# Sums of squares in the mixer: one float32 product, or two rounded ones

## The reference

```python
def l2_normalize(t):
    tf = t.astype(jnp.float32)
    return tf * lax.rsqrt(jnp.sum(tf * tf, axis=-1, keepdims=True) + NORM_EPS)

gdn_qkv = jax.nn.silu(causal_dwconv(gdn_qkv, gdn_conv_w))
g_q, g_k, g_v = [t.reshape(Bsz, S, GDN_HEADS, GDN_HEAD_DIM) for t in jnp.split(gdn_qkv, 3, axis=-1)]
g_q = l2_normalize(g_q) * (GDN_HEAD_DIM ** -0.5)
g_k = l2_normalize(g_k)
# then k k^T and q k^T by chunks of 64 tokens, a triangular inverse of 64x64 blocks, and a scan over 4 chunks
```

## Time and profile before

| | |
|---|---|
| median of 3 runs | 1473.48 us (1473.37 to 1474.0) |
| the profiled execution's own time | 1473.31 us |
| its span | 1471.5 us |
| TensorE busy | 1462.2 us (99%) |
| VectorE, ScalarE, GpSimd busy | 956.8 (65%), 822.2 (56%), 216.1 (15%) |
| granted TensorE clock, mean | 0.998 |
| the four old products of a layer start at | 219.07, 221.34, 231.75, 234.02 (layer 0), 755.41 for the first of layer 1 |
| gram products start at | 241.80 and 778.14 |

### The profile page before, as it was taken

One profiled execution on the slowest core, in us unless ns is written; L12 is line 12 of the kernel. 1 busy time (PEld: TensorE's weight loads), 2 busy tenths in 40 slices (PEclk: granted clock), 3 DMA queues, 4 the chain that ended last, 5 costly groups with the idle time before them and its releaser, 6 DMA issues.

```text
span 1471.5 us, 29397 instructions
## 1 busy us (share of the span) xinstructions
PE 1462.2 (99%) x12785; PEld 1414.7 (96%) x12785; DVE 956.8 (65%) x1394; ACT 822.2 (56%) x1268; POOL 216.1 (15%) x126
## 2 busy tenths in 40 slices
PE   9999999999999999999999999999999999999998
PEld 9999999999999989999999999999989999999997
DVE  6655377786655475655558685655478767677766
ACT  6554377655544365544476655554476675565762
POOL 1000143113000261000332040000430001400001
PEclk9999999999999999999999999999999999999999
DMA  9655464237555456555553256555555344653341
GB/s 384 243 196 184 166 229 144 99 107 263 183 197 201 164 216 229 200 186 190 199 177 140 69 200 218 189 201 196 176 215 201 115 144 166 209 189 139 132 156 58
DMA packets 40239, 267.43 MB, mean 182 GB/s; under 512 B 4464, under 2 KB 4976, under 8 KB 10032
## 3 DMA queue, kind: packets, MB, share of 16 engines
q1 hardware_dynamic: 38592, 260.39, 49.9%
q0 software_dynamic: 944, 4.38, 0.8%
q10 hardware_dynamic: 576, 0.79, 0.2%
HBM read 264.49 MB, written 1.05 MB: 180 GB/s over the span
## 4 chain that ended last, share of the span: by engine, by line
PE 98%; DVE 1%; DMA 0%; ACT 0%; POOL 0%; issue 0%; SPq 0%
PE PS L602 19%; PE PS L604 19%; PE PS L603 19%; PE PS L596 6%; PE PS L598 6%; PE PS L597 6%; PE PS L636 4%; PE PS L635 4%; PE PS L638 4%; PE PS L676 1%; PE PS L1321 1%; PE PS L1044 1%; PE PS L1339 1%; PE PS L1331 1%; PE PS L1352 1%; PE PS L1361 0%
## 5 line engine op out<-in xcount | busy, mean ns | idle before, releaser
L602 PE MATMUL PS<-xTH,WH 128*128 128x256 f32 x2256 | 637.8, 283 | 0.0
L604 PE MATMUL PS<-xTH,rawL 128*128 128x256 f32 x2256 | 624.9, 277 | 0.0
L603 PE MATMUL PS<-xTL,WH 128*128 128x256 f32 x2256 | 624.9, 277 | 0.0
L2065 DVE TENSOR_TENSOR rawL<-raw,WH 128x1024 fp32r<-128x1024 f32 (+1 forms) x407 | 495.0, 1243 | 104.7 <-ACT WH L1488 103.8
L1488 ACT ACTIVATE WH<-raw 128x1024 fp32r<-128x1024 f32 (+2 forms) x477 | 484.5, 1046 | 133.5 <-PE PS L638 98.1
L602 PEld LDWEIGHTS PS<-xTH,WH 128*128 128x128 f32 x2256 | 423.9, 188 | 7.8 <-issue 5.3
L603 PEld LDWEIGHTS PS<-xTL,WH 128*128 128x128 f32 x2256 | 423.8, 188 | 2.6 <-issue 1.9
L604 PEld LDWEIGHTS PS<-xTH,rawL 128*128 128x128 f32 x2256 | 424.5, 188 | 0.0
L2767 POOL TENSOR_TENSOR rawL<-raw,WH 128x1024 fp32r<-128x1024 f32 (+3 forms) x71 | 166.7, 2375 | 767.7 <-ACT WH L1488 767.7
L1568 ACT ACTIVATE sg<-PS 128x256 f32<-128x256 f32 x79 | 30.3, 383 | 168.2 <-PE PS L604 168.2
L635 PE MATMUL PS<-WH,hTH 128*128 128x256 f32 x512 | 122.4, 276 | 0.0
(11 more groups left out here) (424 smaller groups left out, 2183.5 us busy)
## 6 DMA issues: line engine op xcount, KB each, us to landing
raw<-in_weights SPq DMA_DIRECT2D x232, 1024.0 KB, 4.8
gb<-in_lngb SPq DMA_DIRECT2D x16, 512.0 KB, 5.3
raw<-in_weights SPq DMA_DIRECT2D x2, 1056.0 KB, 4.9
raw<-in_weights SPq DMA_DIRECT2D x4, 512.0 KB, 5.4
gb<-in_ln SPq DMA_DIRECT2D x4, 512.0 KB, 4.9
cst<-in_consts POOLq DMA_DIRECT2D x1, 1378.5 KB, 10.0
raw<-in_weights SPq DMA_DIRECT2D x4, 256.0 KB, 5.0
xt<-in_x POOLq DMA_DIRECT2D x1, 1024.0 KB, 17.5
```

The lines of the kernel that those rows point to most:

```text
L602: e.matmul(out, u.H(i, c0, 128), xH, start=first, stop=False)
L603: e.matmul(out, u.H(i, c0, 128), xL, start=False, stop=False)
L604: return e.matmul(out, u.L(i, c0, 128), xH, start=False, stop=end)
L2065: e.tensor_tensor(u.L(i, 0, w), u.R(i, w), u.H(i, 0, w).bitcast(F32), ALU.subtract).then_inc(*low_dve.up(k))
```

## The change

The squares are split like the weights. ScalarE copies `sq` rounded to `sqH` (`square_high`), VectorE subtracts `sq - sqH` into `sqL` (`square_low`), and TensorE multiplies ones (rounded, `onesF`, cast once per layer by VectorE) by sqH and then by sqL into the same bank. The order moves too: on TensorE the four `squares` stand two, three, one and two quarters later; on ScalarE `norm("q", 1)` stands ahead of `rounds("v", 0, 2)` instead of behind it.

```diff
@@ -363,7 +363,8 @@
     decay_act, decay_vec, decays_summed = [signal(n) for n in ("decay_act", "decay_vec", "decays_summed")]
     conv_begun, conv_done, conv_act = [signal(n) for n in ("conv_begun", "conv_done", "conv_act")]
     masks, level_masked = signal("masks"), signal("level_masked")
-    squares_summed, norm_scale, unit_length = [signal(n) for n in ("squares_summed", "norm_scale", "unit_length")]
+    squares_high, squares_low, squares_summed, norm_scale, unit_length = [
+        signal(n) for n in ("squares_high", "squares_low", "squares_summed", "norm_scale", "unit_length")]
     gram_product, gram_masked, tokens_turned, tokens_scaled = [
         signal(n) for n in ("gram_product", "gram_masked", "tokens_turned", "tokens_scaled")]
     inverse_product, inverse_copied, inverse_updated = [signal(n) for n in ("inverse_product", "inverse_copied", "inverse_updated")]
@@ -458,6 +459,9 @@
         m.kq = put("kq", [128, 4, 2, S], 0)
         m.cv = [put("cva", [128, 2, S], 8), put("cvb", [128, 2, S], 10)]
         m.sq = [put("sqa", [128, 512], 12), put("sqb", [128, 512], 14)]
+        m.sqH = [put("sqHa", [128, 512], 44, F32R), put("sqHb", [128, 512], 46, F32R)]
+        m.sqL = [put("sqLa", [128, 512], 48, F32R), put("sqLb", [128, 512], 50, F32R)]
+        m.onesF = put("onesG", [128, 128], 52, F32R)
         m.rs = [put("rsa", [128, 512], 16), put("rsb", [128, 512], 61)]
         m.eb = put("eb", [128, 2, 4, 128], 18)
         m.Es, m.Eu, m.df = [put(n, [128, 8, 64], k) for n, k in (("Es", 22), ("Eu", 24), ("df", 26))]
@@ -898,7 +902,7 @@
         def mix(p, nxt, l):
             m = mix_buffers(l)
             s = ring[0]
-            kq, cv, sq, U, T, Z, Bs, Eu, wq, ez, zb = m.kq, m.cv, m.sq, m.U, m.T, m.Z, m.Bs, m.Eu, m.wq, m.ez, m.zb
+            kq, cv, U, T, Z, Bs, Eu, wq, ez, zb = m.kq, m.cv, m.U, m.T, m.Z, m.Bs, m.Eu, m.wq, m.ez, m.zb
 
             def A(key, off, *freed_by):
                 bank[key] = order[(s + off) % 4]
@@ -983,8 +987,9 @@
 
             def squares(nm, i, b):
                 B(("squares", l, nm, i), b, (norm_scale, (l, nm, i, "ln")))
-                e.wait_ge(*conv_act.at((l, nm, i, "sq")))
-                e.matmul(PS[:, b, :], ones, sq[i][:, :], start=True, stop=True).then_inc(*squares_summed.up((l, nm, i)))
+                e.wait_ge(*squares_low.at((l, nm, i)))
+                e.matmul(PS[:, b, :], m.onesF[:, :], m.sqH[i][:, :], start=True, stop=False)
+                e.matmul(PS[:, b, :], m.onesF[:, :], m.sqL[i][:, :], start=False, stop=True).then_inc(*squares_summed.up((l, nm, i)))
 
             for q in range(3):
                 quarter("k", 1, q)
@@ -992,20 +997,22 @@
             quarter("q", 0, 0)
             quarter("q", 0, 1)
             quarter("q", 0, 2)
+            quarter("q", 0, 3)
+            quarter("q", 1, 0)
             squares("k", 0, 7)
-            quarter("q", 0, 3)
-            squares("k", 1, 4)
-            quarter("q", 1, 0)
             quarter("q", 1, 1)
             quarter("q", 1, 2)
+            squares("k", 1, 4)
             quarter("q", 1, 3)
             quarter("v", 0, 0)
             quarter("v", 0, 1)
             quarter("v", 0, 2)
+            quarter("v", 0, 3)
             squares("q", 0, 5)
-            quarter("v", 0, 3)
+            quarter("v", 1, 0)
+            quarter("v", 1, 1)
             squares("q", 1, 6)
-            for q in range(4):
+            for q in range(2, 4):
                 quarter("v", 1, q)
             quarter("z", 0, 0)
 
@@ -1692,6 +1699,10 @@
                     e.wait_ge(*squares_summed.at((l, "k", i)))
                 e.activation(m.sq[i][:, :].rearrange("p (j s) -> p j s", j=2), dst, ACT.Square).then_inc(*conv_act.up((l, nm, i, "sq")))
 
+            def square_high(nm, i):
+                e.wait_ge(*conv_act.at((l, nm, i, "sq")))
+                e.activation(m.sqH[i][:, :], m.sq[i][:, :], ACT.Copy).then_inc(*squares_high.up((l, nm, i)))
+
             def norm(nm, i):
                 r = m.rs[i]
                 e.wait_ge(*squares_summed.at((l, nm, i)))
@@ -1722,22 +1733,26 @@
             rounds("k", 1, 2)
             conv_end("k", 0)
             conv_first("k", 1)
+            square_high("k", 0)
             rounds("q", 0, 0)
             conv_end("k", 1)
             rounds("q", 0, 2)
             conv_first("q", 0)
+            square_high("k", 1)
             rounds("q", 1, 0)
             conv_end("q", 0)
             rounds("q", 1, 2)
             conv_first("q", 1)
+            square_high("q", 0)
             rounds("v", 0, 0)
             conv_end("q", 1)
+            square_high("q", 1)
             table(TBL_LN_EXP)
             norm("k", 0)
             norm("k", 1)
             norm("q", 0)
+            norm("q", 1)
             rounds("v", 0, 2)
-            norm("q", 1)
             rounds("v", 1, 0)
             rounds("v", 1, 2)
             rounds("z", 0, 0)
@@ -2293,6 +2308,10 @@
                     ins = e.scalar_tensor_tensor(v, v, 128 ** -0.5, r3, op0=ALU.mult, op1=ALU.mult)
                 ins.then_inc(*unit_length.up((l, nm, i)))
 
+            def square_low(nm, i):
+                e.wait_ge(*squares_high.at((l, nm, i)))
+                e.tensor_tensor(m.sqL[i][:, :], m.sq[i][:, :], m.sqH[i][:, :].bitcast(F32), ALU.subtract).then_inc(*squares_low.up((l, nm, i)))
+
             def decayed_q(t):
                 e.wait_ge(*unit_length.at((l, "q", 1)))
                 e.tensor_tensor(m.eb[:, t, :, :], m.eb[:, t, :, :], kq[:, :, 1, 128 * t:128 * t + 128], ALU.mult)
@@ -2312,6 +2331,7 @@
                     *tokens_scaled.up((l, "k", t)))
 
 
+            e.tensor_copy(m.onesF[:, :], ones)
             lows("k", 0, 0)
             lows("k", 0, 2)
             e.wait_ge(*decays_summed.at(l))
@@ -2333,13 +2353,17 @@
             lows("k", 1, 0)
             lows("k", 1, 2)
             conv("k", 1)
+            square_low("k", 0)
             lows("q", 0, 0)
             lows("q", 0, 2)
+            square_low("k", 1)
             conv("q", 0)
             lows("q", 1, 0)
             lows("q", 1, 2)
             conv("q", 1)
+            square_low("q", 0)
             lows("v", 0, 0)
+            square_low("q", 1)
             unit_norm("k", 0)
             unit_norm("k", 1)
             unit_norm("q", 0)
```

## The result

The changed kernel takes 1475.88 us (median of 22 runs, 1475.22 to 1476.66) against 1473.32 for the kernel before on the same chip (22 runs, one of which took 4173.26 us and doesn't move the median): ratio 1.0018, 95% interval 1.0012 to 1.0024. The forecast was 1475.8. So the change costs some 2.6 us (0.18%), though by the forecast's price it takes 3.2 us of work off TensorE. The profiled execution takes 1476.25, its span 1474.1 (before: 1473.31 and 1471.5).

The account below looks back on a forecast made before the run. TensorE bounds the kernel (98% of the chain of waits), but late operands outweigh its gain: 1473.31 + 0.46 (layer 0) + 1.95 (layer 1) = 1475.7 profiled, 1475.9 timed; predicted 1475.8, own range 1475.0 to 1476.9, 8 in 10 within 1472.6 to 1477.6.

Parts of the forecast that it names:

- conv(q0): ScalarE's convolution start for q0, behind k1's rounding and subtraction: +1.27 us in layer 0, +2.61 in layer 1.
- conv_first(q1): ScalarE's first convolution step of q1, layer 0: an earlier wait for TensorE absorbs 0.50 us, +0.77 is left.
- table load: ScalarE's load, behind which all four norms stand, delayed by q1's rounding copy: +1.43 us layer 0, +2.75 layer 1.
- mask of the gram product: VectorE's mask behind its remainders ahead of the inverse: +0.82 us in layer 0, +2.31 in layer 1.
- first product of the inverse: TensorE's start after waiting for GpSimd's first level mask: +0.46 us in layer 0, +1.95 in layer 1.
- TensorE's gain: Eight sums of squares: a pair of rounded matmuls costs 0.47 us in place of 0.87, 3.2 us off TensorE.
- GpSimd in the way: VectorE's subtraction from two SBUF tiles stands until GpSimd's remainder ends, finishes 0.55 us later, lasting 1.8 to 2.2.
- Rival B: The subtraction isn't held by GpSimd: layer 0 stays at +0.46 us, layer 1 loses 0.63, total 1474.6; chance 20%.
- The pauses: TensorE standstills: 1.6 us at squares(q,0), layer 0; 0.6 at squares(k,1), 1.15 at squares(q,0), 1.3 at the gram product, layer 1.
- Rival A: No wait bites and TensorE's whole gain of 3.2 us stays: 1470.2 us; chance 10%.
- Rival C: TensorE's standstills lower its clock to 1.2 GHz; two us of work per layer at that level give 1477.8; chance 8%.
- D: The product's price was mis-sized or the restart is cheaper, so half the delay goes: 1474.0 to 1475.0 us; chance 12%.

Follow-up runs that it names:

- e10: Changed kernel with cast earlier, masks first, k1 behind the convolution, squares in PSUM and GpSimd's chunks counted from the mixer's first: 1469.47 us, ratio 0.9979 to the kernel before.
- e1m: Changed kernel without the splitting work (rounded squares multiplied twice), second norm of q ahead of a remainder, one remainder behind T: 1469.73 us, 0.9978 of the kernel before.
- e3: Changed kernel with the float32 squares written to the PSUM bank of their sum, where copy and subtraction read them: 1474.33 us, 1.0006 of the kernel before.
- e6: Changed kernel with VectorE's subtraction for k1 behind conv(q,0), TensorE's sum of k1 two quarters later, of q0 one: 1471.92 us, 0.9993 of the kernel before.
- e1: Changed kernel without the splitting work: ScalarE writes rounded squares and TensorE multiplies them twice; cast and orders stay: 1470.45 us, 0.9981 of the kernel before.
- e4: Changed kernel with the cast of the ones moved earlier in the phase, into a gap of VectorE: 1474.56 us, 1.0014 of the kernel before.
- e5: Changed kernel with the second norm of q ahead of a remainder on VectorE and one more remainder behind T: 1474.75 us, 1.0012 of the kernel before.
- e2: Changed kernel with GpSimd's chunks counted from the mixer's own first one, so layer 1 alternates as layer 0: 1473.78 us, 1.0006 of the kernel before.
- e8: Changed kernel with all three orders (cast earlier, masks first, k1 behind the convolution), squares still in SBUF: 1470.67 us, 0.9984 of the kernel before.
- e9: Changed kernel with all three orders (cast earlier, masks first, k1 behind the convolution) and squares in PSUM: 1470.01 us, 0.9983 of the kernel before.

## Why the prediction was right

The steps, with the shift of each start against the first product of the decay sums:

| step | forecast | measured |
|---|---|---|
| conv(q0), layer 0 / 1 | +1.27 / +2.61 | +1.26 / +2.64 |
| conv_first(q1), layer 0 | +0.77 | +0.75 |
| table load, layer 0 / 1 | +1.43 / +2.75 | +1.39 / +2.76 |
| mask of the gram product, layer 0 / 1 | +0.82 / +2.31 | +0.78 / +2.30 |
| first product of the inverse, layer 0 / 1 | +0.46 / +1.95 | +0.46 / +1.99 |

The last row of layer 0 is right to the hundredth because two misses of 0.04 cancel: the mask came earlier by that much, and TensorE starts 0.14 to 0.15 us behind the end of what it waited for, not 0.10. In layer 1, where the mask was right, the second one shows.

**TensorE's gain.** A pair without a wait is 0.469 us between the starts around it in e10 (0.47 forecast). e1m shows 1.7 us a layer in place of 1.6; the 0.1 is not in the pair but in the tiles behind: in the kernel before 30 tiles of a layer's stretch stand behind an old product at the longer of two distances, 0.118 for 0.113 us (last section). Behind a wait the pair takes 0.54 (221.69 to 222.23), 0.07 more, which the sum didn't have.

**GpSimd in the way.** The three subtractions named for it lasted 2.12, 2.10 and 2.06 us (1.8 to 2.2 forecast) and end 0.55 behind GpSimd, as the step has it; k0 of layer 1 came later beside it and lasted 1.74. Rival B, not held, is out: with two SBUF sources 0.69 was seen only where GpSimd was idle, and e3 has the form that would behave as B says. Its stages in e3 (44.84 and 45.01) are what B would have cost, 0.35 and 0.52 over before; B's 0.63 for layer 1 was near. By the section "SBUF: two separate sides" of the Trainium skill's page "SBUF — State Buffer" the loser is fully blocked. The traces agree: beside GpSimd 2.08 us with two SBUF sources (e6), 0.68 with a PSUM source (e3).

**The pauses** were right in place and mostly too large: 1.40 for 1.6 at q0 of layer 0, 0.63 for 0.6, 0.80 for 1.15 and about 1.1 for 1.3 in layer 1. One of 0.24 at k0 of layer 0 was missing. In layer 0 TensorE still reached the gram product 0.28 us later than before (36.58 against 36.30 from the start of the measure), where the forecast had 0.1. Its gain of 1.70 is taken back by 1.64 of pauses, 0.14 for the two pairs behind them and 0.21 for 48 tiles behind these at the longer distance; the last two weren't in the forecast. None of this changes the sum, since the chain over ScalarE, VectorE and GpSimd sets the end in both layers; a shorter pause ahead only makes the wait for the level mask longer. e6 moved the end because it took the wait out of ScalarE's chain.

**Rival A**, no wait bites, would have needed the orders of e10. Its 1470.2 is 0.22% under the kernel before, and e10 is 0.21% under it: the price of the products was right, and the waits made the difference. **Rival C** did not come: after pauses up to 1.4 us the granted clock shows its full level, 2.4 GHz, in every slice. The Trainium skill, page "TensorE: Matmul & The Clock Gate", section "Part 1: The HAM clock gate", has the clock drop to half after idling; after these pauses the trace shows no drop. **D** is out by the stages.

**The total** was 1475.88 for 1475.8. The forecast's own sum gives 1475.9, and as a difference it said +2.3 where +2.56 was measured. Between the profiled executions the difference is 2.94 us (own times), of which 2.61 is span, and the steps give 2.45. The spans by stretch differ by -0.34 us ahead of the first decay product, by +1.65 from there to the second layer's (0.46 of it in the stage), and by +1.30 behind (1.99 of it in the stage). What is left, -0.34, +1.19 and -0.69, lies away from the edit, in identical instructions.

The other 0.33 lies outside the span, and it comes with the split. Own time less span is 1.76 to 1.89 us in every execution of e1, of e1m and of the kernel before beside the experiments, which don't split, and 2.12 to 2.26 in every execution of the nine kernels that do. This 0.36 on average was not in the forecast; what it consists of stays open, since it is not in the traces. It also makes part of the difference between e1m, 3.6 us under the kernel before, and e10, 2.6 under it, whose stages are alike. That the median fell so near the forecast is partly luck; that the stages did is not.

## What to carry to other kernels

Taking work off the bounding engine pays only as far as the next operand is early; read that margin (here 0.46 us at one mask) from the timelines before counting the gain. When a sum is split into rounded parts, put the rounding and the subtraction behind, not ahead of, the instruction from which another engine's chain starts, and keep a source of the subtraction in PSUM if GpSimd works at the same time. Here the order was worth more (1.03 and 2.48 us of the two stages, e6) than the source (0.11 and 1.47, e3), since the hold moves on to the next instruction with two SBUF sources. Check each layer: the same order of work met GpSimd differently in the second, because chunks were dealt out by their absolute number.

## What the runs showed of the hardware that was not expected

**Two distances between tile matmuls at full clock.** TensorE's timeline at the same place of the program, kernel before (first fence) and after (second), a high x high product and the one twelve matmuls behind it:

```profile
574.98 0.28 PE L602 MATMUL PS<-xTH,WH 128*128 128x256 f32 x1
...
576.34 0.28 PE L602 MATMUL PS<-xTH,WH 128*128 128x256 f32 x1
```

```profile
574.87 0.28 PE L606 MATMUL PS<-xTH,WH 128*128 128x256 f32 x1
...
576.29 0.28 PE L606 MATMUL PS<-xTH,WH 128*128 128x256 f32 x1
```

Twelve matmuls in 1.36 us there, in 1.42 here: 0.113 and 0.118 us each, with the same recorded duration and the same granted clock. Stretches at the longer distance last microseconds to tens of microseconds.

Around the squares the traces show where such stretches begin. TensorE's timeline after, layer 0, the next pair behind the one at 221.69:

```profile
222.23 0.28 PE L606 MATMUL PS<-xTH,WH 128*128 128x256 f32 x1
...
225.06 0.40 PE L991 MATMUL PS<-sqHb,onesG 128*128 128x512 f32 x1
```

These are 24 tiles in 2.83 us, 0.118 each; ahead of the pause they are 0.113 apart, and from the second tile behind the pair at 225.06 again. Over the eleven kernels with pairs, 20 pairs stand behind a pause (0.10 to 1.42 us), and behind 14 of these at least 24 tiles follow at the longer distance; behind the 68 pairs without a pause it is never more than a tile or two. In the kernel before, the tiles behind each old product are at it. So a pause can cost more than its own length: about 0.07 us in the pair, and up to 0.27 in the tiles behind (59 of them at k1 of layer 1). Why six of the 20 don't start a stretch, and why one ends, stays open.

Elsewhere these stretches begin and end differently from kernel to kernel, without an edit near. In the feed-forward part behind layer 0's mixer the kernel before, e4, e5 and e10 left the longer distance at 559 to 561 us, the other eight (after, e1, e1m, e2, e3, e6, e8, e9) at 591 to 594, which is the 1.2 us above. At the start of the program the kernel before left it at 35 us, the changed one at 18. From 1284 to 1304 us the kernel before is at it, and so, at the same place of the program, are e1 and e1m, but none of the nine kernels that split. The causes stay open. It limits what spans can tell: under about 1 us only a stretch around the edit does.

**A held instruction ends a fixed time after the release, and the time goes with its size**: 0.54 to 0.56 us for 512 columns (24 subtractions), 1.08 to 1.09 for 1024 (the remainders, among them that of the earlier trace rows), in both about 0.13 less than its free duration.
